# The delta rule of a two-block model kernel: four chunks of 64 tokens solved one by one, or two tiles of 128 joined by a corner of the inverse

## The reference, cut to what matters

```
a_low = where(strict, (kb @ k^T) * decay, 0);  ia = a_low + eye(64)
u = solve(ia, v * beta);   w = solve(ia, kb * exp(gc))
def step(state, inp):
    v_new = u_n - w_n @ state
    o_n = qg_n @ state + qk_n @ v_new
    state = state * gl_n + kd_n^T @ v_new
```

## Time and profile before

| | us |
|---|---|
| median of 3 runs | 876.65 (876.02 to 877.37) |
| the profiled execution, its own time | 874.65 |
| its span, from the first to the last instruction | 872.8 |
| PE busy | 859.9 (99% of the span) |
| DVE busy | 582.7 (67%) |
| ACT busy | 440.1 (50%) |
| POOL busy | 53.0 (6%) |

### The profile page before, as it was taken

The page is one execution under the profiler, slowest core; times in us unless marked ns, Lnnn a source line. Parts: engine busy times, 40 slices in busy tenths (PEclk is TensorE's granted clock), DMA queues, the critical chain, the costliest instruction groups (busy, mean ns, idle before and its releaser), DMA issues.

```text
span 872.8 us, 13420 instructions
## 1 busy us (share of the span) xinstructions
PE 859.9 (99%) x5446; PEld 746.4 (86%) x5446; DVE 582.7 (67%) x882; ACT 440.1 (50%) x646; POOL 53.0 (6%) x81
## 2 busy tenths in 40 slices
PE   8999999999999999999999999999999999999997
PEld 6888999898899888888889998768888888888885
DVE  5785664664556656565686998876477677777544
ACT  6654434564355544544475652456353655555342
POOL 1000000000020110000020014200000100000000
PEclk9999999999999999999999999999999999999999
DMA  9757754455555554456748783312555556665541
GB/s 292 251 182 211 230 174 144 125 165 181 159 185 173 174 184 154 165 196 193 277 111 267 194 163 110 134 50 50 145 194 191 192 180 186 192 192 193 169 169 48
DMA packets 124771, 151.61 MB, mean 174 GB/s; under 512 B 15991, under 2 KB 87926, under 8 KB 124710
## 3 DMA queue, kind: packets, MB, share of 16 engines
q1 hardware_dynamic: 124426, 150.41, 54.9%
q10 hardware_dynamic: 220, 0.28, 0.1%
q0 software_dynamic: 64, 0.07, 0.0%
HBM read 148.63 MB, written 3.68 MB: 175 GB/s over the span
## 4 chain that ended last, share of the span: by engine, by line
PE 91%; DVE 3%; ACT 2%; SPq 2%; DMA 1%; issue 1%; POOLq 0%; POOL 0%; ACTq 0%; DVEq 0%
PE bank L525 19%; PE bank L527 19%; PE bank L526 19%; PE bank L1325 9%; PE bank L551 5%; PE bank L1326 5%; PE bank L552 3%; DMA ring<-in_w_mem_kv 1%; PE bank L743 1%; DVE w_lo L2116 1%; PE bank L723 1%; PE bank L983 1%; SPq L1406 1%; PE bank L821 1%; DVE arena L2351 1%
## 5 line engine op out<-in xcount | busy, mean ns | idle before, releaser
L2116 DVE TENSOR_TENSOR w_lo<-ring,w_hi 128x2048 fp32r<-128x2048 f32 (+2 forms) x134 | 298.0, 2228 | 132.3 <-ACT w_hi L1532 132.0
L1532 ACT ACTIVATE w_hi<-ring 128x2048 fp32r<-128x2048 f32 (+2 forms) x134 | 248.9, 1859 | 105.4 <-PE bank L527 78.1
L1325 PE MATMUL bank<-h_both,w_hi 128*128 128x512 f32 x352 | 122.7, 393 | 0.2 <-issue 0.2
L525 PE MATMUL bank<-h_both,w_hi 128*128 128x256 f32 x424 | 122.4, 289 | 0.0
L526 PE MATMUL bank<-h_both,w_hi 128*128 128x256 f32 x424 | 119.9, 283 | 0.0
L527 PE MATMUL bank<-h_both,w_lo 128*128 128x256 f32 x424 | 119.9, 283 | 0.0
L1326 PE MATMUL bank<-h_both,w_lo 128*128 128x256 f32 x352 | 98.5, 280 | 0.0
L525 PE MATMUL bank<-w_hi,h_both 128*128 128x512 f32 (+2 forms) x224 | 86.1, 384 | 0.0
L527 PE MATMUL bank<-w_hi,h_both 128*128 128x512 f32 (+2 forms) x224 | 84.1, 375 | 0.0
L526 PE MATMUL bank<-w_lo,h_both 128*128 128x512 f32 (+2 forms) x224 | 84.0, 375 | 0.0
L525 PEld LDWEIGHTS bank<-h_both,w_hi 128*128 128x128 f32 x424 | 81.3, 192 | 1.4 <-issue 1.1
(11 more groups left out here) (385 smaller groups left out, 1509.3 us busy)
## 6 DMA issues: line engine op xcount, KB each, us to landing
ring<-in_w_in SPq DMA_DIRECT2D x59, 1024.0 KB, 5.1
ring<-in_w_gate_up SPq DMA_DIRECT2D x44, 512.0 KB, 4.7
ring<-in_w_down SPq DMA_DIRECT2D x10, 1024.0 KB, 5.0
ring<-in_w_mem_kv SPq DMA_DIRECT2D x8, 1024.0 KB, 10.2
ring<-in_w_gla_out SPq DMA_DIRECT2D x4, 1024.0 KB, 5.1
ring<-in_w_x_out SPq DMA_DIRECT2D x4, 1024.0 KB, 5.2
ring<-in_w_dsa_out SPq DMA_DIRECT2D x4, 1024.0 KB, 5.2
ring<-in_w_o SPq DMA_DIRECT2D x4, 1024.0 KB, 5.1
```

Of the source, the lines that this page charges most:

```text
L525: mm(o, ah, bh, start=start, stop=False, skip_group_check=True)
L1325: mm(o[:, :], wh[:, k - k0, w], h_both[:, :, k, :], start=k == 0, stop=False, skip_group_check=True)
L1532: act(w_hi[:, k % NHI, at:m], ring[:, order.index(name) % NSLOT, at:m], ACT.Copy)\
L2116: tt_(w_lo[:, i, at:m], ring[:, i, at:m], w_hi[:, k % NHI, at:m].bitcast(F), ALU.subtract)\
```

## The change: what it does

The two chunks of a tile are treated as one system of 128 tokens. Its inverse has the two 64x64 inverses on its diagonal and one corner between them, which `corner_first` and `corner_second` compute (`lz6`, `xt6`) from a product of the later chunk's keys with the earlier one's (`of`). `new_values(t)` (`dn`) then solves a whole tile: the first 64 tokens from the first inverse, the last 64 from corner and second inverse together. One state is left, between the tiles: `gdn_state` (`gs`) and `keys_of_state` (`ks`), whose result DVE subtracts from the values of the second tile (`values_left`). `gdn_out(t)` makes the outputs of one tile. The transposed keys of the second tile, `kbe`, `u`, `w` and three of the state steps are gone. The caps `ahead[0]` of ACT and DVE and the order of their steps around the gate units change with it. ACT's copies of the levels and NSA up to step 13 stay as they are, and `z_half(3)` stays ahead of `level_end(5)`.

The core of the diff (left out: names of tiles, the removed bodies, small scale columns made on GpSimd ahead of the levels):

```diff
-            head_transposes("kk", 4)
+            bank = open_bank("kk0")
+            for h in range(4):
+                ins = nc.tensor.transpose(bank[:, 128 * h:128 * h + 128], cv[:, 4 + h, 0:128], ident)
+            done("kk0", ins)
+            pe.wait_ge(signal("q_decayed"), 1)
+            for t in range(TT):
+                bank, first, second = open_bank(f"of{t}"), slice(128 * t, 128 * t + 64), slice(128 * t + 64, 128 * t + 128)
+                for h in range(4):
+                    mm(bank[64:128, 64 * h:64 * h + 64], cv[:, 4 + h, second], cv[:, 4 + h, first], start=True, stop=True)
+                    ins = mm(bank[0:64, 64 * h:64 * h + 64], cv[:, 4 + h, first], egc[:, h, second], start=True, stop=True)
+                done(f"of{t}", ins)
...
+            def corner_first():
+                for t in range(TT):
+                    pe.wait_ge(*read(f"xt5{t}"))
+                    pe.wait_ge(*read(f"of{t}"))
+                    bank = open_bank(f"lz6{t}")
                     for h in range(4):
...
+                        i = 4 * t + h
+                        ins = mm(bank[0:64, 64 * h:64 * h + 64], crossed[64:128, i, :], TmT[64:128, i, :], start=True, stop=True)
+                    done(f"lz6{t}", ins)
+
+            def corner_second():
+                pe.wait_ge(signal("T_turned"), 6)
+                for t in range(TT):
+                    pe.wait_ge(*read(f"lz6{t}"))
+                    bank = open_bank(f"xt6{t}")
+                    for h in range(4):
+                        i = 4 * t + h
+                        ins = mm(bank[0:64, 64 * h:64 * h + 64], Tm[0:64, i, :], zst[0:64, i, :], start=True, stop=True)
+                    done(f"xt6{t}", ins)
+
+            def new_values(t):
+                pe.wait_ge(*read(f"xt6{t}"))
+                pe.wait_ge(signal("corner"), 1)
+                if t == 1:
+                    pe.wait_ge(*read("ks"))
+                bank = open_bank(f"dn{t}")
                 for h in range(4):
-                    ins = mm(bank[:, 128 * h:128 * h + 128], kdt[:, 4 * t + h, :], v_new[c % 2][:, 4 * t + h, :],
+                    i, at = 4 * t + h, slice(128 * h, 128 * h + 128)
+                    mm(bank[0:64, at], TmT[0:64, i, :], vb[0:64, i, :], start=True, stop=True)
+                    ins = mm(bank[64:128, at], corner[:, i, :], vb[:, i, :], start=True, stop=True)
+                done(f"dn{t}", ins)
...
+            def gdn_state():
+                pe.wait_ge(*read("dn0"))
+                bank = open_bank("gs")
+                for h in range(4):
+                    ins = mm(bank[:, 128 * h:128 * h + 128], kdt[:, h, :], v_new[:, h, :], start=True, stop=True)
+                done("gs", ins)
+
+            def keys_of_state():
+                pe.wait_ge(*read("gs"))
+                bank = open_bank("ks")
+                for h in range(4):
+                    ins = mm(bank[:, 128 * h:128 * h + 128], cv[:, 4 + h, 128:256], gstate[:, 128 * h:128 * h + 128],
                              start=True, stop=True)
-                done(f"gs{c}", ins)
+                done("ks", ins)
...
+            def gdn_out(t):
+                pe.wait_ge(*read(f"dn{t}"))
+                pe.wait_ge(signal("qk_masked"), 2)
+                if t == 1:
+                    pe.wait_ge(signal("q_decayed"), 2)
+                bank = open_bank(f"gd{t}")
+                for h in range(4):
+                    i, at = 4 * t + h, slice(128 * h, 128 * h + 128)
+                    mm(bank[0:64, at], qkT[0:64, i, :], v_new[0:64, i, :], start=h == 0, stop=t == 0, skip_group_check=True)
+                    ins = mm(bank[64:128, at], crossed[:, i, :], v_new[:, i, :], start=h == 0, stop=t == 0, skip_group_check=True)
+                    if t == 1:
+                        mm(bank[0:64, at], egc[:, h, 128:192], gstate[:, at], start=False, stop=True, skip_group_check=True)
+                        ins = mm(bank[64:128, at], q_second[:, h, :], gstate[:, at], start=False, stop=True, skip_group_check=True)
+                done(f"gd{t}", ins)
...
+            corner_first()
+            nsa_transposes(15)
+            corner_second()
+            nsa_out(3)
...
-            gdn_state(0)
-            gate_part("mb0", 0, lambda: gdn_chunk(1))
-            gdn_state(1)
-            gate_part("mb0", 1, lambda: gdn_chunk(2))
-            gdn_state(2)
-            gate_part("mb1", 0, lambda: gdn_chunk(3))
-            gdn_out()
+            gate_part("mb0", 0, lambda: new_values(0))
+            gdn_state()
+            gate_part("mb0", 1, keys_of_state)
+            gdn_out(0)
+            new_values(1)
+            gate_part("mb1", 0)
+            gdn_out(1)
             gate_part("mb1", 1)
...
-            for i in range(12, 15):
-                nsa_step(i)
+            nsa_step(12)
+            nsa_step(13)
             ahead[0] = splits.index("mb0a") + 1
             highs(ahead[0])
...
+            nsa_step(14)
+            nsa_copy(15)
+            for t in range(TT):
+                copy(f"xt6{t}", corner[0:64, 4 * t:4 * t + 4, :],
+                     bank_of(f"xt6{t}")[0:64, 0:256].rearrange("p (a b) -> p a b", a=4))
+            nsa_high(3)
...
-            for c in range(2):
-                copy(f"wt{c}", wT[:, :, 64 * c:64 * c + 64], bank_of(f"wt{c}")[:, :].rearrange("p (a b) -> p a b", a=8))
-            nsa_step(15)
+            copy("dn0", v_new[:, 0:4, :].rearrange("p a b -> p (a b)"))
+            copy("gs", gstate)
             ahead[0] = len(splits)
             merge_gate("mb0")
+            copy("dn1", v_new[:, 4:8, :].rearrange("p a b -> p (a b)"))
...
             for n in range(2, 6):
                 level_mask(n)
-            gp.wait_ge(*full("lz51"))
-            nc.gpsimd.memset(v_new[0][64:128, :, :], 0.0).then_inc(signal("v_zero"), 1)
-            gp.wait_ge(*full("xt51"))
-            nc.gpsimd.memset(v_new[1][0:64, :, :], 0.0).then_inc(signal("v_zero"), 1)
+            gp.wait_ge(*read("xt51"))
+            nc.gpsimd.tensor_scalar(corner[64:128], TmT[64:128], 1.0, None, ALU.mult).then_inc(signal("corner"), 1)
+            gp.wait_ge(*full("lz61"))
+            nc.gpsimd.tensor_scalar(crossed[64:128], qkT[64:128], 1.0, None, ALU.mult).then_inc(signal("qk_masked"), 1)
+            gp.wait_ge(signal("qk_masked"), 2)
+            gp.wait_ge(signal("q_decayed"), 1)
+            nc.gpsimd.tensor_tensor(q_second, egc[:, :, 192:256], chunk_decay[:, :, 2:3].broadcast_to([128, 4, CH]), ALU.mult)\
+                .then_inc(signal("q_decayed"), 1)
...
+            bank_ready("kk0")
+            ve.wait_ge(signal("state_cols"), 1)
+            tt_(kdt, by_head("kk0"), col4(0, 28), ALU.mult).then_inc(reader("kk0"), 1)
+            ve.wait_ge(signal("between_cols"), 1)
+            for t in range(TT):
+                bank_ready(f"of{t}")
+                tt_(crossed[:, 4 * t:4 * t + 4, :], by_chunk(f"of{t}"), col4(t, 12, CH), ALU.mult).then_inc(reader(f"of{t}"), 1)
...
                 if n < 5:
-                    for t in range(TT):
-                        ve.wait_ge(*read(f"xt{n}{t}"))
                     turned(Tm, TmT)
+                else:
+                    nc.vector.transpose(Tm[32:64, :, 0:32], TmT[0:32, :, 32:64]).then_inc(signal("T_turned"), 1)
...
+            def corner_scaled():
+                for t in range(TT):
+                    bank_ready(f"lz6{t}")
+                    s, rows = slice(4 * t, 4 * t + 4), bank_of(f"lz6{t}")[0:64, 0:256].rearrange("p (h c) -> p h c", h=4)
+                    tt_(zst[0:64, s, :], rows, cols[0:64, t, 8:12].unsqueeze(2).broadcast_to([64, 4, CH]), ALU.mult)\
+                        .then_inc(reader(f"lz6{t}"), 1)
+
+            def values_left():
+                bank_ready("ks")
...
+                    ins = stt(vb[:, 4 + h, :], bank_of("ks")[:, 128 * h:128 * h + 128], cols[:, 1, 28 + h:29 + h],
+                              vb[:, 4 + h, :], ALU.mult, ALU.add)
+                ins.then_inc(reader("ks"), 1)
...
-            ve.wait_ge(signal("q_decayed"), 1)
-            chunk_new(0)
+            corner_scaled()
+            ahead[0] = splits.index("mb0a") + 1
+            lows(ahead[0])
...
-            ahead[0] = splits.index("mb0a") + 1
+            ahead[0] = splits.index("mb0b") + 1
             lows(ahead[0])
             low_of_out(3)
-            for c in range(NCH - 1):
-                chunk_state(c)
-                ahead[0] += 1
-                chunk_new(c + 1)
+            values_left()
```

More of the change, by code:

```diff
@@ L318, in build @@
         alpha, soft, g_tok = (tiled(log_at + 8 * i, TT, 4) for i in range(3))
[L319 removed]
+        kdt, vb = tiled(raw_at, 4, 128), tiled(cv_at + 2048, 8, 128)
         nA, qkT = tiled(nA_at, 8, CH), tiled(qkT_at, 8, CH)
@@ L323, in build @@
         gd_rows = tiled(nA_at, 8, 128)
-        gstate = [flat(cv_at + 512 * i, 512) for i in range(3)]
-        u_tok, wT = tiled(zst_at, 8, 128), tiled(nAm_at[0], 8, 128)
-        v_new = (tiled(nAm_at[1], 8, 128), tiled(Tm_at, 8, 128))
```

(36 more changed lines are left out.)

44 lines of the change are left out of this document (8 added, 36 removed).

## The result

| | before | changed |
|---|---|---|
| median of the runs | 877.01 us (876.02 to 878.25, 4 runs) | 888.18 us (887.28 to 889.28, 4 runs) |
| profiled execution: time, span | 874.65, 872.8 us | 887.28, 885.5 us |

The changed kernel is slower: 1.0127 of before, 95% interval 1.0109 to 1.0145, 11.2 us by the medians. I had forecast 885.2; the case that came true is the rival in which the clock falls in the new wait, 887.9.

What follows compares the result with a forecast made beforehand. PE, busy 99% of the span, was taken as the bound. PE work +4.4, wait gone -0.9, new wait +5.0 give +8.5 us; 876.65 + 8.5 = 885.2 us, range 880.0 to 888.4.

Steps and rivals of the forecast that it cites:

- the rival in which the clock falls in the new wait: PE's idle time before `mb0b` halves its clock, work behind it runs slower: +2.7 us, 887.9; chance 0.18.
- The price of a change of part: On PE, each change of array part between matmuls costs 0.145 us, the same in both directions.
- The alternating blocks: `dn0`, `gd0` with `dn1`, and `gdn_out(1)`: 7.85 us of matmuls plus 5.1 of changes of part, together 12.95.
- alternating is free: In `dn` and `gd`, changes of part hide behind queued matmuls: 7.7 us less, 877.5; chance 0.10, free or nearly.
- The wait that goes: `nsa_out(3)` on PE runs without waits, 1.9 us instead of 2.79, saving 0.9; `mb0a`'s split stays hidden.
- The wait that comes: PE idles 5.0 us before `mb0b`, whose rounding stands behind the copy of `gs` on ACT, then DVE's rest.
- The split isn't late: Before `mb0b`, PE's wait is over when `gs` ends: 5.0 us less, 880.2; chance 0.06.
- Upstream: Ahead of level 5's end PE has 0.8 us more work: four transposes 0.44, `of` 1.23, less 0.87 for `kk`.

Runs made afterwards that it cites:

- e2: Changed kernel with the four 64*64 products of each block ahead of the 128*64 ones, same matmuls: 883.43 us, 1.0082 of before.
- e1: Changed kernel with ScalarE rounding `mb0b` before it copies `dn0` instead of after the copy of `gs`: 880.39 us, 1.0042 of before.
- e5: Changed kernel with both halves side by side and zeros, one 128*128 product per head and operand in `dn` and `gd`: 878.66 us, 1.0018 of before.
- e4: Changed kernel with 21 added products right behind `gs`, so TensorE works through its wait before `mb0b`: 885.94 us, 1.0103 of before.
- e3: Changed kernel with the 64*64 products of `dn` and `gd` taken over all 128 rows, some results wrong: 880.03 us, 1.0034 of before.
- e6: Changed kernel with both the 128*128 products for `dn` and `gd` and the early rounding of `mb0b`: 871.98 us, 0.9944 of before.

## Why the prediction was nearly right, and where it was short

| step (us) | forecast | trace |
|---|---|---|
| shift before level 5's end (`kk0`, `of`) | +0.8 | +0.42, not resolved |
| `u`, `w`, `nsa_out(3)`, `gs0` out of the front, `lz6`, `xt6` in | -3.5 | -3.5 |
| blocks `dn`, `gd`, `gs`, `ks` for `ws`, `gs`, `gdn_out` | +6.2 | +6.5 |
| gate halves behind a change of part | 0 | +0.3 |
| wait before `mb0b` | +5.0 | +4.8 |
| clock behind the wait | 0 (rival: 2.7) | +2.05 |
| sum | +8.5 | +10.5 |

The front is 604.95 - 595.38 = 9.57 in before's timeline and 601.86 - 595.80 = 6.06 in the changed kernel's. The blocks are 2.89 + 5.77 + 3.76 + 1.05 + 0.81 = 14.28 now (1.05 is `gs` to the start of the wait); before they were 3.78 and five of 0.81 (the first from 607.77 to 608.57 in its timeline), 7.8. In the forecast's own terms, with 0.81 for `gs`, the blocks are +6.2 and the wait is 5.05 (from 611.39 to 616.44): both as forecast.

- *The price of a change of part* held: 0.145 forecast, 0.143 measured in e2. In `dn0` both directions between the two parts cost alike, 0.36 a matmul in every step, as assumed. The alternating blocks took 12.42 us against 12.95. The rival "alternating is free" needed under 0.02 a change.
- *The wait that goes*: `nsa_out(3)` took 601.86 - 599.98 = 1.88, forecast 1.9; `mb0a` waits for nothing.
- *The wait that comes*: place, releaser and chain as told. Of its links the rounding took 1.93 (612.16 to 614.09; 1.87 forecast) and the rest 2.29 (2.28). One link was misread: 0.27 is the whole of one record and not "what one record takes beyond its pitch" (1.03 - 8 x 0.109 = 0.16); the pitch is taken off at the end of that sum, so that the 5.0 holds.
- *The split isn't late*: out, by the trace and by e1.
- *Upstream*: the 0.8 can't be tested by the trace. Level 5 ends at 595.64 to 596.60 in the seven variants, which have the changed kernel's code up to there but for the strided tiles, and at 595.38 and 597.57 in two executions of before.
- *The step that was short*: the sum had the clock behind the wait at nothing, and the rival that had it got a weight of 0.18. Measured, the term is 2.05. What I held against it, "up to 870 the row still shows 1.00, well after the last matmul", was no argument: the earlier trace rows has the fall in the same idle time, only later. The price of 2.7 was too high: 4.93 - 2.88 is 2.05, and in e5, where the pace was full again sooner, 4.45 - 2.82 is 1.6. The Trainium skill, "TensorE: Matmul & The Clock Gate", Part 1, has the rule that an idle TensorE is gated to half its clock, and e4 agrees with it: without the idle time the clock stays. With this term the forecast would have been 887.3.
- The median, 888.18, lies 1.0 above 876.65 + 10.5. The profiled execution, 887.28, is 0.1 above it; the other 0.9 is within the 2.0 by which the changed kernel's runs spread. So that the median comes within 0.3 of the clock rival's 887.9 is partly luck: the rival's price was 0.65 too high, and the place of the median in the spread made up for it.

## What to carry to other kernels

Count changes of array part as you count matmuls: two triangular halves as 64*64 and 128*64 in turn cost 0.72 us a pair, the same data with zeros as one 128*128 product 0.20 to 0.22. When a change moves an engine's copy behind a product, look at what its queue holds behind that copy and who waits for it, and move that work into idle time further up. An idle time of TensorE of nearly 5 us cost 7 here, since the work behind it began at the lower clock. Compare two profiles over the stretch of the change, not by a place on the clock of the whole span: two executions of the same kernel differed by 2.2 us ahead of it.

## What the runs showed of the hardware that was not expected

GpSimd's copy of `crossed` took 3.43 us, where the copy of `corner`, of the same shape, took 1.50; VectorE's rest of `mb0a` ran in the meantime, at its usual length. The timelines of POOL and DVE in the changed kernel:

```profile
597.51 1.50 POOL L2114 TENSOR_SCALAR arena<-arena 64x512 f32<-64x512 f32 x1 [25.28 <-DVE arena L2715]
599.09 3.43 POOL L2116 TENSOR_SCALAR arena<-arena 64x512 f32<-64x512 f32 x1
...
598.88 2.27 DVE L2155 TENSOR_TENSOR w_lo<-ring,w_hi 128x2048 fp32r<-128x2048 f32 x1
```

e1 and e3 have the same 3.43. In e6 a fill of 0.52 stands ahead of the copy, the copy overlaps VectorE's rest (599.35 to 601.62) by 1.48 us in place of 2.06, 0.58 less, and takes 2.85, 0.58 less. The copy of `corner` overlaps the rest by 0.13 (598.88 to 599.01). In all three the copy takes 1.37 more than the overlap, as if GpSimd stood still beside this subtraction of two tiles in SBUF; no run took the overlap away altogether. Not all of VectorE's work does it: beside `corner`'s copy VectorE also ran a transposition (0.43) and two products with a bank (0.88), with one input in SBUF each, and e6's fill takes 0.52 beside the rest and 0.52 later without it. The Trainium skill, "SBUF — State Buffer", "Who interferes with whom", has this rule: a VectorE instruction with two inputs in SBUF contends with a GpSimd instruction that reads SBUF, and not with one that only writes it. It cost nothing here, since `crossed` was wanted 23 us later (602.52, and `gd0` at 625.45).
